# The two residual writes of a layer norm on GpSimd: after both token blocks are normalised, and not one by one

## What is computed

```
for every sublayer f (8 of them):
    r = alpha * h + scale * f(h)            # scale 0.5 or 1
    h = (r - mean(r)) * rsqrt(var(r) + 1e-5) * g + b
```

## Time and profile before

| | us |
|---|---|
| median of 3 runs | 1572.83 |
| lowest, highest | 1572.08, 1573.27 |
| the profiled execution, whole | 1570.33 |
| its span (first to last instruction) | 1568.5 |
| TensorE busy in the span | 1545.2 |
| VectorE busy | 944.7 |
| ScalarE busy | 735.0 |
| GpSimd busy | 129.2 |

### The profile page before, as it was taken

The page is one execution under the profiler, slowest core; times in us unless marked ns, Lnnn a source line. Parts: engine busy times, 40 slices in busy tenths (PEclk is TensorE's granted clock), DMA queues, the critical chain, the costliest instruction groups (busy, mean ns, idle before and its releaser), DMA issues.

```text
span 1568.5 us, 21643 instructions
## 1 busy us (share of the span) xinstructions
PE 1545.2 (99%) x8804; PEld 1337.9 (85%) x8804; DVE 944.7 (60%) x925; ACT 735.0 (47%) x673; POOL 129.2 (8%) x149
## 2 busy tenths in 40 slices
PE   8999999999999999999999999999999999999997
PEld 7888888788888988889878898898999788888886
DVE  5555565565556655566457655557586456775555
ACT  5454455344445444443334444445536556453442
POOL 1000011110001000023121200002003200020000
PEclk9999999999999999999999999999999999999999
DMA  8554554255554655465454465456444335455551
GB/s 302 188 188 178 197 214 163 108 188 188 185 197 154 235 191 190 170 220 203 171 181 148 164 228 188 173 202 229 151 161 162 109 133 188 153 197 188 191 195 69
DMA packets 41723, 283.88 MB, mean 181 GB/s; under 512 B 4912, under 2 KB 5232, under 8 KB 8752
## 3 DMA queue, kind: packets, MB, share of 16 engines
q1 hardware_dynamic: 37728, 270.55, 47.3%
q0 software_dynamic: 2368, 8.59, 1.6%
q10 hardware_dynamic: 1552, 3.64, 0.7%
HBM read 281.65 MB, written 1.05 MB: 180 GB/s over the span
## 4 chain that ended last, share of the span: by engine, by line
PE 93%; DVE 3%; ACT 2%; POOL 1%; issue 1%; DMA 0%; POOLq 0%; ACTq 0%; DVEq 0%
PE psum L1421 20%; PE psum L1424 20%; PE psum L1425 19%; PE psum L1524 16%; PE psum L1528 8%; PE psum L1466 1%; PE psum L1453 1%; PE psum L1459 1%; PE psum L1433 1%; PE psum L1740 1%; DVE weights_lo L882 1%; ACT squares L433 1%; POOL att_p L386 1%; DVE normalised L874 0%; DVE weights_lo L828 0%
## 5 line engine op out<-in xcount | busy, mean ns | idle before, releaser
L828 DVE TENSOR_TENSOR weights_lo<-weights_raw,weights_hi 128x2048 fp32r<-128x2048 f32 x249 | 574.8, 2319 | 382.7 <-ACT weights_hi L413 380.7
L413 ACT ACTIVATE weights_hi<-weights_raw 128x2048 fp32r<-128x2048 f32 (+1 forms) x256 | 483.6, 1890 | 350.1 <-PE psum L1425 211.5
L1524 PE MATMUL psum<-operand,weights_hi 128*128 128x512 f32 x1088 | 258.6, 390 | 0.0
L1421 PE MATMUL psum<-operand,weights_hi 128*128 128x256 f32 x864 | 246.1, 285 | 0.3 <-DVE weights_lo L828 0.3
L1424 PE MATMUL psum<-operand,weights_hi 128*128 128x256 f32 x864 | 244.4, 283 | 0.0
L1425 PE MATMUL psum<-operand,weights_lo 128*128 128x256 f32 x864 | 244.4, 283 | 0.0
L1524 PEld LDWEIGHTS psum<-operand,weights_hi 128*128 128x128 f32 x1088 | 202.1, 188 | 40.5
L1421 PE MATMUL psum<-weights_hi,hidden_hi 128*128 128x512 f32 x480 | 188.1, 392 | 0.2
L1424 PE MATMUL psum<-weights_lo,hidden_hi 128*128 128x512 f32 x480 | 187.6, 391 | 0.0
L1425 PE MATMUL psum<-weights_hi,hidden_lo 128*128 128x512 f32 x480 | 186.9, 389 | 0.0
L1421 PEld LDWEIGHTS psum<-operand,weights_hi 128*128 128x128 f32 x864 | 165.7, 192 | 3.6 <-issue 2.2
(11 more groups left out here) (266 smaller groups left out, 1582.9 us busy)
## 6 DMA issues: line engine op xcount, KB each, us to landing
weights_raw<-in_weights SPq DMA_DIRECT2D x256, 1024.0 KB, 4.8
ln_rows<-in_ln_rows POOLq DMA_DIRECT2D x16, 512.0 KB, 5.4
normalised<-in_x SPq DMA_DIRECT2D x2, 512.0 KB, 6.5
ret_constants<-in_ret_constants ACTq DMA_DIRECT2D x1, 1024.0 KB, 4.8
out<-normalised SPq DMA_DIRECT2D x4, 256.0 KB, 2.0
att_constants<-in_att_constants ACTq DMA_DIRECT2D x1, 576.0 KB, 5.0
gla_w_low<-in_gla_w_low ACTq DMA_DIRECT2D x1, 512.0 KB, 3.5
att_w_small<-in_att_w_small ACTq DMA_DIRECT2D x1, 512.0 KB, 3.8
```

Of the source, the lines that this page charges most:

```text
L413: nc.scalar.activation(w_hi[:, s, whole], raw[:, s, whole], ACT.Copy).then_inc(hi_split, 1)
L828: nc.vector.tensor_tensor(w_lo[:, s, :], raw[:, s, :], w_hi[:, s, :].bitcast(F32), ALU.subtract).then_inc(lo_split, 1)
L1421: mm(out, a_hi, b_hi, start=start, stop=False, skip_group_check=True)
L1524: mm(work[:, b, :], w_hi[:, slot, cols], x_both[:, c, :, :].rearrange("p a t -> p (a t)"), start=c == 0, stop=False, skip_group_check=True)
```

## The change

GpSimd waits once, for `xn_ready` of 4 ln (all four halves normalised), ahead of both residuals; before, it waited for the two halves of block 0 ahead of `residual(0)` and for all four ahead of `residual(1)`. It applies to the seven layer norms with `ln < 8`. Nothing else differs.

```diff
                 if ln < 8:
+                    pool.wait_ge(xn_ready, 4 * ln)
                     for tb in range(TB):
-                        pool.wait_ge(xn_ready, 4 * (ln - 1) + 2 * tb + 2)
                         residual(tb, ALPHA if ln < 6 else ALPHA_2)
                     load_rows(ln + 1)
```

## The result

| | before | changed |
|---|---|---|
| median of 6 runs each, us | 1572.55 | 1564.95 |
| lowest, highest | 1570.12, 1573.27 | 1564.08, 1565.33 |
| profiled execution, whole | 1570.33 | 1565.12 |
| its span | 1568.5 | 1563.3 |

A forecast was written before the change was run, and what follows sets the result against it. TensorE, busy 1545.2 of 1568.5 us, bounds the kernel; its waits for line 882 cost 5.5 us. Seven gains of 0.83 us make 5.8, so 1572.83 - 5.8 = 1567.0 us, range 1564.0 to 1569.5.

The forecast's parts named there:

- The first residual leaves line 882: VectorE's second w_lo piece falls from 1.52 to 0.69 us; 0.83 us gained per layer norm, 5.8 us over seven.
- How the two block each other: GpSimd's first residual waits until normalise ends, then line 882 waits for that residual; each blocks the other whole.
- TensorE is ready when the piece comes: Line 1466 can start at 508.99 instead of 509.82, transposes being done; 0.83 us taken, 0.79 the lower end.
- What TensorE meets earlier: Matmuls of lines 1453 and 1459 and the second half's transposes move 0.83 us earlier, without a new wait.
- The first residual costs the split of line 828 the same 0.47 us: At its new place it delays VectorE's whole-tile split as the other residual did; row stays at 2.76 us.
- The second residual lets the split go first: VectorE's waiting line 828 goes between the residuals; the second residual's row becomes some 3.1 us, with nobody waiting.
- rival A: Second residual goes ahead of line 828's split; TensorE waits 0.3 us at line 1459; 1569.1 us; chance 6%.
- Lines 973 in the first and the sixth: VectorE's subtraction may meet the second residual's end; done at 208.69, TensorE wants it at 208.86: hidden by 0.15 us.
- Rival B: The residual was not what held line 882, which keeps 1.5 us; time stays at 1572.8 us; chance 4%.
- Rival C: GpSimd runs residuals and row loads as one block before line 828's split; slower, 1577.3 us; chance 3%.
- The sum: 5.8 us less: 1564.5 us against the profiled execution, 1567.0 us against the median, 0.37% less.

The follow-up runs named there:

- the other order: Both residuals in one GpSimd instruction of 128x2048, against the changed kernel: 1567.33 us, changed kernel beside it 1565.41; ratio to before 0.9966.

## Why the prediction was right, and where it was short

- *The first residual leaves line 882*: right. 0.83 us per layer norm was the term, 0.82 to 0.86 is what the distances show, 5.87 against 5.8 in all.
- *How the two block each other*: right in kind. The forecast says that the residual does not get on until `normalise` ends; by its own numbers (509.23 less 1.06) it gets on at 508.17, 0.16 us before the recorded end at 508.33, as line 882 does behind the residual. No term of the sum uses it.
- *TensorE is ready when the piece comes*: right. It starts line 1466 at 508.03, 0.05 us behind the end of the piece, and shows no idle time for it; the weight loads show the 0.2 us that were left.
- *What TensorE meets earlier*: right, the two waits for `normalise` and for `rows_lo` move along.
- *The first residual costs the split of line 828 the same 0.47 us*: right, 2.75 us.
- *The second residual lets the split go first* (rows 8 against rival A): right. The merged row of 4.09 us has the second residual at 3.09 (the longest of line 314), where 3.1 was forecast. The price of the other order was about right: 1.9 us by the medians and 2.7 by the traces, where 2.1 was forecast; it left out that line 973 would then be late as well.
- *Lines 973 in the first and the sixth*: hidden, 109.44 us to the next layer norm against 109.40.
- *Rival B*: fell with the 684 to 694 ns of line 882. *Rival C*: fell; the loads of the gain rows, now at 513.55, hold up nothing.
- *The sum* was short by 1.8 us of 7.6 against the median, inside the range. The step that was mis-sized is the one from the profiled execution to the median: the forecast took the 2.5 us between the two as something that the change would leave alone (1572.83 - 5.8). Against the profiled execution it says 1564.5, and 1564.95 was measured. The clocks on record show why: that execution was one of the few of before without a fall, most have a lower clock, and the changed kernel's do not. A term of 0 to 1.55 us more, one fall of the clock, was missing. The range held the result because its lower end was reckoned from that fast execution, not because the forecast had a reason for the median to come there.

## What to carry to other kernels

Two instructions that overlap on VectorE and GpSimd and are both longer than usual are blocked by each other: compare them with a free instruction of the same shape, and the excess is the price. Moving the GpSimd instruction is worth that price only where VectorE's instruction is waited for; here 0.83 us counted at one line and 0.47 us at another counted for nothing. Two short GpSimd instructions leave VectorE a gap that one long one does not (line 828 at 2.75 us against 3.70). A GpSimd instruction that only fills a tile held up nothing here: `normalise` took 0.75 us beside it and 1.63 behind a residual write.

## What was not expected of the hardware

- The granted clock fell to half for about 3.4 us in two of four traces in which TensorE had stood for about 0.97 and then 0.80 us, and did not in the other two with the same idle times; each fall cost 1.55 us. Where the fall goes with the wait, taking 0.86 us of wait away gives 2.4 us.
- A fall of the same length came in two traces at about 1236 us, where TensorE's rows, by their modelled ends, show no idle time before it.
- Which of two instructions that start 0.05 us apart gets on first can turn: of the 28 layer norms in traces with the old order, one had GpSimd first. The delay was nearly the same (0.88 and 0.83 us).
